# The down projections in square blocks, with Strassen's seven products in two of eleven super-groups

## The chip, the core and the metric

The kernel runs on one core of one Trainium2 chip. The time is the device time of one execution in microseconds (us). TensorE multiplies matrices, VectorE (DVE) and ScalarE (ACT) work on elements, GpSimd (POOL) does elementwise work too, and SyncE (SP) issues the loads. SBUF is the on-chip memory of 128 partitions, PSUM holds TensorE's results, and weights come from DRAM.

## The reference, cut to what matters

Two transformer blocks of width 2048 follow each other on 256 tokens: attention and a gated feed-forward network (1), then a gated recurrence and a gated feed-forward network (2), all in float32. The change is in the two down projections, the last products of the networks:

```
D_MODEL = 2048
SEQ = 256
D_FF = 5632
...
        u = causal_dwconv(h @ w_up[l], conv_w[l], conv_b[l])
        gate, up = jnp.split(u, 2, axis=-1)
        y = (jax.nn.gelu(gate, approximate=True) * up) @ w_down[l]
        x = x + rms_norm(y, post_ffn_norm[l])
...
    up = dwconv3(h @ w_in, w_conv)
    gate, val = jnp.split(up, 2, axis=-1)
    return (jax.nn.silu(gate) * val) @ w_out
```

So y (256 x 2048) is the hidden matrix (256 x 5632) times the weights (5632 x 2048). Its rows are normalised afterwards, which needs the sum of squares over all 2048 columns of a token.

## The kernel before, in words

The eight phases are called in1, out1, up1, down1, in2, out2, up2 and down2. All of them stream float32 weights in chunks of 256 rows and 512 columns (`raw`, 128 x 1024 elements, 512 KB) through a ring of four slots. Each chunk n is loaded by SP (`load`, L207), copied by ACT to `whi` (`split_hi`, L214, type fp32r), and VectorE writes the rest, raw minus whi, to `wlo` (`split_lo`, L219). TensorE then multiplies in three terms, high by high, high by low and low by high: for each of two 128-row tiles (`k`) and two token tiles (`t`) three matmuls of 128x512 output, twelve in a chunk (`products`, L232 to L234).

Four semaphores tie this together. A load into a slot waits until `lo_done` says that wlo of the chunk four before is done. `split_hi` waits until the chunk has landed and until `chunk_used` says that TensorE has used chunk n-4. `split_lo` waits for `hi_done`, and TensorE waits for `lo_done`.

A down projection has four groups of 512 output columns. For each group TensorE goes through all 44 row tiles (22 chunks) and gathers in one of two accumulators `acc` (256 tokens x 512 columns, one PSUM bank for each token tile). While the next group runs in the other accumulator, VectorE scales the finished group by the norm's gain row into `ybuf` (`back_group_dve`, L481) and ACT squares it and sums the squares (`back_group_act`, L489); then `group_free` says that the accumulator is free. The last four chunks of the last group go by token (`last_products`, L404 to L406): all of token tile 0 (`token0`), then all of token tile 1. `last_act` (L419, L423) squares and takes the root, VectorE takes the reciprocal (L444), scales the last group (L438), and adds each piece to `x` (L537). After down1, `pre_pe_by_token` turns `x` for in2 (L318, L306), with transposes for filling (L295). After down2, `x` goes to the output.

The hidden matrix comes from the up projection, one super-group of 512 hidden columns after the other, eleven in all, 44.2 us each. ACT copies the halves out (L589), VectorE scales them (`evacuate` L644, `scaled` L649), ACT starts the convolution of three taps (`centre`, L598: gate half in `cvg`, up half in `cvu`), VectorE adds the other taps (`convolve`, L662), ACT applies gelu or silu (L604), and POOL multiplies `cvg` by `cvu` (L718) and splits the product into `hhi` (L720) and `hlo` (L722). `centre` of super-group i waits until POOL is done with super-group i-1 (`up_hid`). The work of the last super-group lies in the first steps of the down projection.

The order of the work of each engine is the order in which the code is written; nothing is scheduled at run time except by semaphores.

## Time and profile before

| | |
|---|---|
| median of 3 runs | 2511.09 us (2509.42 to 2518.72) |
| the profiled execution: its span | 2510.2 us |
| the profiled execution's own time beside its span | none is listed apart from the span; the span is 0.9 us under the median |
| TensorE busy | 2496.8 us (99%), 15417 matmuls |
| VectorE busy | 1656.4 us (66%) |
| ACT busy | 1336.6 us (53%) |
| POOL busy | 221.3 us (9%) |
| DRAM read | 458.40 MB, 183 GB/s over the span |

The busy time of an engine is the union of its instructions. A matmul's duration in the profile (0.39 us for 128x512) is longer than the distance between two starts, since matmuls overlap; what one costs is read from the starts, or from a stretch divided by its count.

### The profile page before, as it was taken

To read this page: it belongs to the slowest core of one execution; us is meant where nothing else is said; L and a number is where in the kernel's file an instruction comes from. 1 tells how busy PE (TensorE), PEld (TensorE's weight loads), DVE (VectorE), ACT (ScalarE), POOL (GpSimd) and SP (SyncE) were. 2 spreads that over 40 slices of the span, in tenths; PEclk is the share of its full clock that TensorE was granted. 3 is DMA by queue.
4 is the path that set the end of the run, shared out by engine and by line. 5 is a ranking of instruction groups with operands and counts; after the bars stand their busy time and mean duration, and the time that the engine had idled before them with its cause. 6 is when DMAs were issued, how large, how long until landed. Compare 5 with 4: busy or idle time off the path is not lost.

```text
span 2510.2 us, 40508 instructions
## 1 busy us (share of the span) xinstructions
PE 2496.8 (99%) x15417; PEld 2153.2 (86%) x15417; DVE 1656.4 (66%) x2020; ACT 1336.6 (53%) x1754; POOL 221.3 (9%) x96
## 2 busy tenths in 40 slices
PE   9999999999999999999999999999999999999998
PEld 9999988888888888888888888888888888888887
DVE  6665675776777775445495968775677777775444
ACT  6554564656565554445545455454656556554343
POOL 1000000031211211000000000000012131221000
PEclk9999999999999999999999999999999999999999
DMA  7865445566666666555655655545566666666554
GB/s 236 254 206 154 118 140 185 180 190 188 189 186 191 192 188 210 195 194 187 193 173 164 176 154 174 160 149 188 174 186 192 191 186 191 188 189 211 194 194 156
DMA packets 241720, 462.25 MB, mean 184 GB/s; under 512 B 14392, under 2 KB 23921, under 8 KB 240961
## 3 DMA queue, kind: packets, MB, share of 16 engines
q1 hardware_dynamic: 239937, 453.45, 58.9%
q0 software_dynamic: 1568, 7.10, 0.9%
q8 instruction: 85, 1.39, 0.2%
q14 instruction: 34, 0.28, 0.0%
q10 hardware_dynamic: 96, 0.02, 0.0%
HBM read 458.40 MB, written 2.12 MB: 183 GB/s over the span
## 4 chain that ended last, share of the span: by engine, by line
PE 98%; ACT 0%; DMA 0%; DVE 0%; issue 0%; SPq 0%; DVEq 0%; ACTq 0%
PE acc L232 13%; PE acc L252 13%; PE acc L233 13%; PE acc L234 13%; PE tp L252 13%; PE tp L254 7%; PE acc L254 7%; PE acc L967 2%; PE acc L969 2%; PE acc L970 2%; PE acc L1193 1%; PE acc L1195 1%; PE acc L1194 1%; PE tp L1696 1%; PE acc L975 1%; PE acc L977 1%
## 5 line engine op out<-in xcount | busy, mean ns | idle before, releaser
L219 DVE TENSOR_TENSOR wlo<-raw,whi 128x1024 fp32r<-128x1024 f32 x855 | 1073.8, 1263 | 725.9 <-ACT whi L214 724.3
L214 ACT ACTIVATE whi<-raw 128x1024 fp32r<-128x1024 f32 x855 | 902.5, 1059 | 991.1 <-PE acc L234 458.2
L252 PE MATMUL acc<-ahl,whi 128*128 128x512 f32 x1408 | 490.2, 392 | 0.6 <-DVE ahl L337 0.6
L252 PE MATMUL tp<-ahl,whi 128*128 128x512 f32 x1408 | 489.5, 391 | 0.0
L254 PE MATMUL tp<-ahl,wlo 128*128 128x256 f32 x1408 | 394.2, 280 | 0.0
L254 PE MATMUL acc<-ahl,wlo 128*128 128x256 f32 x1408 | 394.1, 280 | 0.0
L252 PEld LDWEIGHTS acc<-ahl,whi 128*128 128x128 f32 x1408 | 263.4, 187 | 59.0 <-issue 1.0
L252 PEld LDWEIGHTS tp<-ahl,whi 128*128 128x128 f32 x1408 | 263.3, 187 | 57.7
L232 PE MATMUL acc<-whi,ahl 128*128 128x512 f32 x752 | 298.7, 397 | 1.8 <-DVE ahl L1794 1.5
L234 PE MATMUL acc<-whi,ahl 128*128 128x512 f32 x752 | 293.0, 390 | 0.0
L233 PE MATMUL acc<-wlo,ahl 128*128 128x512 f32 x752 | 292.7, 389 | 0.0
L254 PEld LDWEIGHTS tp<-ahl,wlo 128*128 128x128 f32 x1408 | 266.1, 189 | 0.1
L254 PEld LDWEIGHTS acc<-ahl,wlo 128*128 128x128 f32 x1408 | 266.0, 189 | 0.0
L234 PE MATMUL acc<-whi,hlo 128*128 128x512 f32 x672 | 261.4, 389 | 0.0
L233 PE MATMUL acc<-wlo,hhi 128*128 128x512 f32 x672 | 261.4, 389 | 0.0
L232 PE MATMUL acc<-whi,hhi 128*128 128x512 f32 x672 | 261.4, 389 | 0.0
L718 POOL TENSOR_TENSOR cvg<-cvg,cvu 128x1024 f32<-128x1024 f32 x22 | 98.2, 4462 | 1485.8 <-DVE cvu L662 1485.8
L232 PEld LDWEIGHTS acc<-whi,ahl 128*128 128x128 f32 x752 | 141.2, 188 | 31.4 <-issue 2.8
L234 PEld LDWEIGHTS acc<-whi,ahl 128*128 128x128 f32 x752 | 141.2, 188 | 29.9
L233 PEld LDWEIGHTS acc<-wlo,ahl 128*128 128x128 f32 x752 | 141.3, 188 | 27.5
L967 PE MATMUL acc<-ahl,whi 128*128 128x256 f32 x512 | 151.4, 296 | 0.2 <-DVE wlo L1572 0.2
L234 PEld LDWEIGHTS acc<-whi,hlo 128*128 128x128 f32 x672 | 126.1, 188 | 26.4
(286 smaller groups left out, 2963.8 us busy)
## 6 DMA issues: line engine op xcount, KB each, us to landing
raw<-in_w_up_dram SPq DMA_DIRECT2D x176, 512.0 KB, 4.1
raw<-in_ffn_w_in_dram SPq DMA_DIRECT2D x176, 512.0 KB, 4.2
raw<-in_hgrn_w_in_dram SPq DMA_DIRECT2D x160, 512.0 KB, 3.6
raw<-in_w_down_dram SPq DMA_DIRECT2D x88, 512.0 KB, 3.9
raw<-in_ffn_w_out_dram SPq DMA_DIRECT2D x88, 512.0 KB, 3.7
raw<-in_w_in_dram SPq DMA_DIRECT2D x87, 512.0 KB, 4.1
raw<-in_w_out_dram SPq DMA_DIRECT2D x32, 512.0 KB, 3.6
raw<-in_hgrn_w_out_dram SPq DMA_DIRECT2D x32, 512.0 KB, 3.8
```

Of the source, the lines that this page charges most:

```text
L214: act.activation(whi[:, s, :], raw[:, s, :], ACT.Copy).then_inc(hi_done, 1)
L219: dve.tensor_tensor(wlo[:, s, :], raw[:, s, :], whi[:, s, :].bitcast(F32), ALU.subtract).then_inc(lo_done, 1)
L232: pe.matmul(out[:, t, :], xh, whi[:, s, c], start=(kt == 0), stop=False)
L233: pe.matmul(out[:, t, :], xh, wlo[:, s, c], start=False, stop=False)
L234: mm = pe.matmul(out[:, t, :], xl, whi[:, s, c], start=False, stop=(kt == nk - 1))
L252: pe.matmul(o[:, ct % 2, :].rearrange("p (a t) -> p a t", a=2), whi[:, s, c], ahl[:, :, kt, :], start=(kt == 0), stop=False, skip_group_ch ...
L254: mm = pe.matmul(o[:, ct % 2, 0:S], wlo[:, s, c], ahi[:, kt, :], start=False, stop=(kt == KT - 1), skip_group_check=True)
L718: pool.tensor_tensor(cvg[:, :, :], cvg[:, :, :], cvu[:, :, :], ALU.mult).then_inc(sem(f"{ph}_pr"), 1)
L967: pe.matmul(o[:, d], whi[:, s, a], ahi[:, kt, :], start=first and ct % 2 == 0, stop=False, skip_group_check=True)
L969: pe.matmul(o[:, d], whi[:, s, a], alo[:, kt, :], start=False, stop=False, skip_group_check=True)
L970: mm = pe.matmul(o[:, d], wlo[:, s, a], ahi[:, kt, :], start=False, stop=last, skip_group_check=True)
L975: pe.matmul(out[:, t, :], xh, whi[:, s, a], start=first, stop=False)
```

## The change

The up projections' arithmetic, the attention and the recurrence stay. In a down projection:

- The loops are written out: 100 steps (`DOWN`) instead of 88 chunks. The output is made in two pairs of column groups (i = 0, 1); both accumulators are open at once. Super-groups of 512 hidden rows come in the order 0, 1, 2, 5, 3, 4, 6, 7, 8, 10, 9. One super-group and one pair is a square of 2 x 2 weight chunks (256 rows by 512 columns each).
- Nine super-groups (`R_SGS`) are regular: four steps of twelve matmuls (L552 to L554 of the changed kernel).
- Super-groups 5 and 10 (`S_SGS`) make seven block products, each a step of six matmuls (L566 to L568) with one token tile's worth of hidden blocks. Four of the steps use sums of weight chunks: `weight_sums` (L647) adds them in place in `raw`, two chunks at a time, and each sum is then split again into whi and wlo. A raw slot is free only after the last step that uses it, steps 3 to 6 (`FREED`).
- The hidden side: for these super-groups POOL's `seven_parts` makes the sums of hidden blocks and splits seven blocks, nine operations in place of two. Super-group 10 (`LATE`) goes through `down_pool`, after the load of the gain row.
- Products 1, 5, 6 and 7 gather in the two `tp` pairs of banks; the others go straight into the open accumulators. After super-group 10 ACT copies product 1 (L673), and VectorE forms U (L694), W (L705) and two more differences (L711, L718) and adds them to the four output blocks (L701, L707, L714, L720). The last super-group, 9, waits block by block for these additions (`down_last`): by columns, (token 0, columns 0), (1, 0), (0, 1), (1, 1), or in the last pair of down2 by token, (0, 0), (0, 1), (1, 0), (1, 1). Block 0 is the first of them.
- At the end of down1 and down2 two column groups are scaled, squared and added where there was one (`c1_act`, `c1_y`, `down_rest`).

The core of the diff:

```diff
+S_RAW = (0, 2, 3, 0, 1, 2, 3)
+S_A = (0, 6, 1, 4, 3, 5, 2)
+S_SGS = (5, 10)
...
+LATE = 10
+DOWN_ORDER = (0, 1, 2, 5, 3, 4, 6, 7, 8, 10, 9)
...
+        def back_load(sp, ph, w):
+            for m in range(M_DOWN):
...
+                    sp.wait_ge(lo_done, cb[ph] + FREED[m - RING] + 1)
...
+        def one_of_seven(pe, ph, d):
+
+            out = (P1B, cols(ph, 1)[:, 0, :], cols(ph, 0)[:, 0, :], P5B, P7B, P6B, cols(ph, 0)[:, 1, :])[d.j]
+            a = S_A[d.j]
...
+            for kk in range(CK):
+                w = slice(kk * GC, (kk + 1) * GC)
+                xh, xl = part7(d.sg, 0, a, kk), part7(d.sg, 1, a, kk)
+                pe.matmul(out, xh, whi[:, d.n % RING, w], start=fresh and kk == 0, stop=False, skip_group_check=True)
+                pe.matmul(out, xh, wlo[:, d.n % RING, w], start=False, stop=False, skip_group_check=True)
+                mm = pe.matmul(out, xl, whi[:, d.n % RING, w], start=False, stop=False, skip_group_check=True)
+            mm.then_inc(chunk_used, 1)
...
+            for b, (t, c) in enumerate(blocks_of(i, nxt)):
+                pe.wait_ge(sem("pre_sums"), 4 * (NPAIR * DOWNS.index(ph) + i) + b + 1)
...
+        def down_hi(act, ph, d):
+
+            n = cb[ph] + d.n
+            if d.summed and d.j >= 3:
+                act.wait_ge(sem("sums"), ub[ph] + SUMS[d.i, d.sg] + d.j - 2)
+            else:
+                act.wait_ge(landed[d.m % RING], 16 * ((rb[ph] + d.m) // RING + 1))
+            act.wait_ge(chunk_used, n - RING + 1)
+            act.activation(whi[:, d.n % RING, :], raw[:, d.m % RING, :], ACT.Copy).then_inc(hi_done, 1)
...
+        def weight_sums(dve, ph, d):
...
+            if d.j == 0:
+                dve.wait_ge(landed[1], 16 * ((rb[ph] + d.m + 1) // RING + 1))
+                add(0, 1)
+            if d.j == 1:
+                add(1, 2)
+            if d.j == 2:
+                dve.wait_ge(sem("sums"), s0 + 1)
+                add(2, 0)
+                dve.wait_ge(sem("sums"), s0 + 3)
+                add(3, 2)
...
+                if at == -1:
+                    sum_11(dve, ph, d.i)
+                if at == 1:
+                    sum_u(dve, ph, d.i)
+                    (sum_12 if by_token else sum_21)(dve, ph, d.i)
+                if at == 2 and not by_token:
+                    sum_12(dve, ph, d.i)
+                if at == 3:
+                    if by_token:
+                        sum_21(dve, ph, d.i)
+                        down_rest(dve, ph, k, 0)
+                    sum_22(dve, ph, d.i)
```

VectorE's order in down1 before, from the first chunk after the up projection's tail to the third group's scaling (`x18` is eighteen alike in a row):

```order
L219 TENSOR_TENSOR wlo<-raw,whi 128x1024 x18
L481 TENSOR_TENSOR ybuf<-acc,gbd 128x512 x2
L219 TENSOR_TENSOR wlo<-raw,whi 128x1024 x21
L481 TENSOR_TENSOR ybuf<-acc,gbd 128x512 x2
L219 TENSOR_TENSOR wlo<-raw,whi 128x1024 x23
```

The changed kernel, VectorE in down1, from the first sum of super-group 10 to the first output sums of the first pair:

```order
L647 TENSOR_TENSOR raw<-raw 128x1024
L639 TENSOR_TENSOR wlo<-raw,whi 128x1024
L647 TENSOR_TENSOR raw<-raw 128x1024
L639 TENSOR_TENSOR wlo<-raw,whi 128x1024
L647 TENSOR_TENSOR raw<-raw 128x1024 x2
L639 TENSOR_TENSOR wlo<-raw,whi 128x1024 x4
L701 TENSOR_TENSOR acc<-acc,ybuf 128x512
L639 TENSOR_TENSOR wlo<-raw,whi 128x1024 x2
L694 TENSOR_TENSOR ybuf<-tp,ybuf 128x512
L711 TENSOR_TENSOR ybuf<-tp,ybuf 128x512
L714 TENSOR_TENSOR acc<-acc,ybuf 128x512
L639 TENSOR_TENSOR wlo<-raw,whi 128x1024
```

Four sums of raw (L647) now stand between the wlo of the seven steps, and six more operations of 128x512 between the wlo of super-group 9.

POOL in the up projection's loop before, for one super-group:

```order
L718 TENSOR_TENSOR cvg<-cvg,cvu 128x1024
L720 ISA
L720 COPY hhi<-cvg 128x1024
L722 REGISTER_ALU
L722 TENSOR_TENSOR hlo<-cvg,hhi 128x1024
```

POOL of the changed kernel for super-group 5:

```order
L990 TENSOR_TENSOR cvg<-cvg,cvu 128x1024
L1011 TENSOR_TENSOR cvu<-cvg 128x512
L1013 CAST hsum<-cvg 128x512
L1014 CAST hsum<-cvg 128x256
L1016 TENSOR_TENSOR cvu<-cvg,cvu 128x256
L1018 TENSOR_TENSOR hsum<-cvg,hsum 128x512
L1020 TENSOR_TENSOR hsum<-cvg,hsum 128x256
L1022 TENSOR_TENSOR cvu<-cvg,cvu 128x256
L1024 CAST hsum<-cvu 128x1024
L1026 TENSOR_TENSOR hsum<-cvu,hsum 128x1024
```

The product (L718, now L990) stays, and a copy and a subtract have become nine operations. The same nine follow for super-group 10 after the load of `gbd`.

VectorE at the end of down1, before:

```order
L219 TENSOR_TENSOR wlo<-raw,whi 128x1024 x14
L444 RECIPROCAL prs<-prs 128x1
L537 SCALAR_TENSOR_TENSOR x<-ybuf,prs,x 128x512
L438 TENSOR_TENSOR ybuf<-acc,gbd 128x512
L219 TENSOR_TENSOR wlo<-raw,whi 128x1024
L537 SCALAR_TENSOR_TENSOR x<-ybuf,prs,x 128x512
L219 TENSOR_TENSOR wlo<-raw,whi 128x1024
L444 RECIPROCAL prs<-prs 128x1
L537 SCALAR_TENSOR_TENSOR x<-ybuf,prs,x 128x512
L438 TENSOR_TENSOR ybuf<-acc,gbd 128x512
L537 SCALAR_TENSOR_TENSOR x<-ybuf,prs,x 128x512
```

And in the changed kernel, from the last output sum on:

```order
L720 TENSOR_TENSOR acc<-acc,ybuf 128x512
L725 TENSOR_REDUCE prs<-psq 128x1
L727 TENSOR_SCALAR prs<-prs 128x1
L725 TENSOR_REDUCE prs<-psq 128x1
L727 TENSOR_SCALAR prs<-prs 128x1
L267 TENSOR_TENSOR wlo<-raw,whi 128x1024
L734 TENSOR_TENSOR ybuf<-acc,gbd 128x512 x2
L504 RECIPROCAL prs<-prs 128x1
L799 SCALAR_TENSOR_TENSOR x<-ybuf,prs,x 128x512 x2
L267 TENSOR_TENSOR wlo<-raw,whi 128x1024
L504 RECIPROCAL prs<-prs 128x1
L799 SCALAR_TENSOR_TENSOR x<-ybuf,prs,x 128x512
```

Two reductions by token and two scalings of the third group have moved behind the last wlo, and the first wlo of in2 has moved ahead of the reciprocal of token 0.

## Rows read from the trace of the kernel before

**Rows 1.** The page, part 1: busy us of each engine, share, instructions.

```profile
PE 2496.8 (99%) x15417; PEld 2153.2 (86%) x15417; DVE 1656.4 (66%) x2020; ACT 1336.6 (53%) x1754; POOL 221.3 (9%) x96
```

**Rows 2.** Windows of down1 and down2: span, busy of PE, PEld, DVE, ACT, POOL, PEclk, DMA.

```profile
930.90:1170.30 239.40, 239.40 (x1058) 198.16 (x1057) 118.08 (x109) 101.33 (x110) 9.97 (x4) 1.00 0.59 195
2262.90:2502.70 239.80, 239.76 (x1059) 198.18 (x1057) 118.30 (x111) 98.42 (x107) 9.96 (x4) 1.00 0.55 186
```

**Rows 3.** Timeline of PE and ACT in down1: start us, us, what [idle before, releaser].

```profile
933.66 0.39 PE L232 MATMUL acc<-whi,hhi 128*128 128x512 f32 x1
...
933.92 1.06 ACT L214 ACTIVATE whi<-raw 128x1024 fp32r<-128x1024 f32 x1 [0.73 <-PE acc L234]
...
955.68 1.06 ACT L214 ACTIVATE whi<-raw 128x1024 fp32r<-128x1024 f32 x1 [1.65 <-PE acc L234]
```

**Rows 4.** Timeline of DVE in up1.

```profile
903.60 2.35 DVE L219 TENSOR_TENSOR wlo<-raw,whi 128x1024 fp32r<-128x1024 f32 x2
...
916.89 1.21 DVE L649 TENSOR_TENSOR ut<-ut,uprow 128x1024 f32<-128x1024 f32 x1
```

**Rows 5.** An issue; landings of loads issued at 953.66, 969.51, 1004.41, 958.99.

```profile
955.64 0.37 SPq L207 DMA_DIRECT2D raw<-in_w_down_dram  x1
...
DMA to landing us min/median/max: 3.5/3.5/3.5
...
DMA to landing us min/median/max: 3.8/3.8/3.8
...
DMA to landing us min/median/max: 4.4/4.4/4.4
...
DMA to landing us min/median/max: 8.0/8.0/8.0
```

**Rows 6.** Chain at in2's first matmul, between DVE's ahl and TensorE.

```profile
1174.86 0.14 issue
```

**Rows 7.** Timeline of DVE and ACT at the first group's end in down1.

```profile
993.28 1.28 DVE L481 TENSOR_TENSOR ybuf<-acc,gbd 128x512 f32<-128x512 f32 x2
...
995.79 2.00 ACT L214 ACTIVATE whi<-raw 128x1024 fp32r<-128x1024 f32 x2
```

**Rows 8.** Timeline of POOL and of DVE in the first steps of down1.

```profile
947.97 4.45 POOL L718 TENSOR_TENSOR cvg<-cvg,cvu 128x1024 f32<-128x1024 f32 x1 [34.41 <-DVE cvu L662]
952.60 1.81 POOL L720 CAST hhi<-cvg 128x1024 f32 x1 [0.17 <-POOL cvg L718]
954.57 3.18 POOL L722 TENSOR_TENSOR hlo<-cvg,hhi 128x1024 f32 x1 [0.17 <-POOL hhi L720]
...
947.80 2.36 DVE L219 TENSOR_TENSOR wlo<-raw,whi 128x1024 fp32r<-128x1024 f32 x2
...
951.34 2.16 DVE L219 TENSOR_TENSOR wlo<-raw,whi 128x1024 fp32r<-128x1024 f32 x1 [1.18 <-ACT whi L214]
954.06 1.42 DVE L219 TENSOR_TENSOR wlo<-raw,whi 128x1024 fp32r<-128x1024 f32 x1 [0.56 <-ACT whi L214]
956.78 2.05 DVE L219 TENSOR_TENSOR wlo<-raw,whi 128x1024 fp32r<-128x1024 f32 x1 [1.30 <-ACT whi L214]
```

**Rows 9.** Timeline of DVE and ACT around a super-group's change in up1.

```profile
912.79 1.85 DVE L219 TENSOR_TENSOR wlo<-raw,whi 128x1024 fp32r<-128x1024 f32 x1 [1.50 <-ACT whi L214]
...
922.63 3.47 DVE L662 SCALAR_TENSOR_TENSOR cvg<-ut,taps,cvg 128x255 f32<-128x255 f32 x8
...
918.43 2.08 ACT L598 ACTIVATE cvg<-ut,taps 128x256 f32<-128x256 f32 x4
```

**Rows 10.** Timeline of ACT and DVE at the end of down1.

```profile
1165.77 1.28 ACT L423 ACT_TABLE_LOAD   x1
...
1168.26 0.68 DVE L438 TENSOR_TENSOR ybuf<-acc,gbd 128x512 f32<-128x512 f32 x1
...
1171.98 0.75 DVE L537 SCALAR_TENSOR_TENSOR x<-ybuf,prs,x 128x512 f32<-128x512 f32 x1
```

**Rows 11.** Timeline of DVE at the end of down2.

```profile
2505.22 2.07 DVE L537 SCALAR_TENSOR_TENSOR x<-ybuf,prs,x 128x512 f32<-128x512 f32 x3
```

More of the change, by code:

```diff
@@ new lines, in bass_two_blocks, with blocks_of, part7, regular @@
+        BY_TOKEN = ((0, 0), (0, 1), (1, 0), (1, 1))
+        BY_COLUMNS = ((0, 0), (1, 0), (0, 1), (1, 1))
+        def blocks_of(i, nxt):
+            return BY_TOKEN if i == NPAIR - 1 and not nxt else BY_COLUMNS
+        def part7(sg, lo, a, kk):
+            if sg == LATE:
+                return hlate[:, lo, 2 * a + kk, :]
+            return hsum[:, lo, 2 * a + kk, :]
+        def regular(pe, ph, d):
+            r, c = RC[d.j]
+            for kk in range(CK):
+                kt, w = 4 * R_SGS.index(d.sg) + CK * r + kk, slice(kk * GC, (kk + 1) * GC)
+                first = d.sg == DOWN_ORDER[0] and r == 0 and kk == 0
+                for t in range(NT):
+                    xh, xl = hhi[:, kt, t * P:(t + 1) * P], hlo[:, kt, t * P:(t + 1) * P]
+                    pe.matmul(cols(ph, c)[:, t, :], xh, whi[:, d.n % RING, w], start=first, stop=False, skip_group_check=True)
+                    pe.matmul(cols(ph, c)[:, t, :], xh, wlo[:, d.n % RING, w], start=False, stop=False, skip_group_check=True)
+                    mm = pe.matmul(cols(ph, c)[:, t, :], xl, whi[:, d.n % RING, w], start=False, stop=False,
+                                   skip_group_check=True)
+            mm.then_inc(chunk_used, 1)
@@ new lines, in down_last @@
+        def down_last(pe, ph, i, n, sg, nxt):
+            for b, (t, c) in enumerate(blocks_of(i, nxt)):
+                pe.wait_ge(sem("pre_sums"), 4 * (NPAIR * DOWNS.index(ph) + i) + b + 1)
+                for r in range(2):
+                    s = (n + 2 * c + r) % RING
+                    if t == 0:
+                        pe.wait_ge(lo_done, cb[ph] + n + 2 * c + r + 1)
+                    for kk in range(CK):
+                        kt, w = 4 * R_SGS.index(sg) + CK * r + kk, slice(kk * GC, (kk + 1) * GC)
+                        xh, xl = hhi[:, kt, t * P:(t + 1) * P], hlo[:, kt, t * P:(t + 1) * P]
+                        pe.matmul(cols(ph, c)[:, t, :], xh, whi[:, s, w], start=False, stop=False, skip_group_check=True)
+                        pe.matmul(cols(ph, c)[:, t, :], xh, wlo[:, s, w], start=False, stop=False, skip_group_check=True)
+                        mm = pe.matmul(cols(ph, c)[:, t, :], xl, whi[:, s, w], start=False,
+                                       stop=(r == 1 and kk == CK - 1), skip_group_check=True)
+                    if t:
+                        mm.then_inc(chunk_used, 1)
+                if i == NPAIR - 1 and t == 0:
+                    mm.then_inc(sem("token0") if c else sem("down_c1"), 1)
@@ new lines, in back_pe @@
+        def back_pe(pe, ph, k, ready, nxt):
+            pe.wait_ge(ready, FG)
+            pe.wait_ge(group_free, gb[ph] - 1)
+            for d in DOWN:
+                if d.i and d.sg == DOWN_ORDER[0] and d.j in (0, 2):
+                    group(pe, gb[ph] + 2 * d.i + RC[d.j][1])
+                if d.summed and d.n == DOWN_FIRST_SUM:
+                    pe.wait_ge(group_free, gb[ph])
+                if d.sg == LATE and d.i == 0 and d.j == 0:
+                    pe.wait_ge(ready, FG + 1)
+                if d.last:
+                    if d.j == 0:
+                        down_last(pe, ph, d.i, d.n, d.sg, nxt)
+                else:
+                    pe.wait_ge(lo_done, cb[ph] + d.n + 1)
+                    (one_of_seven if d.summed else regular)(pe, ph, d)
@@ new lines, in down_lo, with add @@
+        def down_lo(dve, ph, d):
+            dve.wait_ge(hi_done, cb[ph] + d.n + 1)
+            dve.tensor_tensor(wlo[:, d.n % RING, :], raw[:, d.m % RING, :], whi[:, d.n % RING, :].bitcast(F32),
+                              ALU.subtract).then_inc(lo_done, 1)
+        def weight_sums(dve, ph, d):
+            s0 = ub[ph] + SUMS[d.i, d.sg]
+            def add(to, other):
+                dve.tensor_tensor(raw[:, to, :], raw[:, to, :], raw[:, other, :], ALU.add).then_inc(sem("sums"), 1)
+            if d.j == 0:
+                dve.wait_ge(landed[1], 16 * ((rb[ph] + d.m + 1) // RING + 1))
[7 more added lines that the diff above has]
+                add(3, 2)
```

323 lines of the change are left out of this document (236 added, 87 removed).

## The prediction

> **What bounds the kernel now.** I read the page first: TensorE is busy 99% of the span, VectorE 66%, ACT 53% [rows 1]. A microsecond saved on TensorE is a microsecond of the result only while its operands keep coming, so the question is what else is nearly late. The stretches that the change rewrites are the two down projections, 930.90 to 1170.30 us and 2262.90 to 2502.70 us. TensorE has no gap in them, and its granted clock is 1.00, the 2.4 GHz level [rows 2]. The first holds 1056 matmuls of its own (1058 less two of the up projection), so one costs 239.4/1056 = 0.227 us, a step of twelve 2.72 us, a step of six 1.36 us.
>
> Then I read how a weight chunk reaches TensorE. ACT copies chunk n to whi once step n-4 has freed the slot, 0.3 us later (step 1 begins at 933.66, the copy at 933.92) [rows 3]; VectorE starts wlo 1.10 us after the copy started (955.68, 956.78) [rows 3, 8]. Two wlo in a row take 2.35 us: 1.23 for one, 1.14 from start to start [rows 4]. The reload of raw is issued 0.15 us after the wlo that frees it (955.48, 955.64). It lands after 3.5 or 3.8 us where the queue had been quiet for over 3 us, after 4.4 in the normal rhythm, and after 8.0 beside the 1 MB gain row [rows 5]. In that rhythm wlo is ready some 5.5 us ahead (three steps of 2.72 less 0.3, less 2.3 from the copy's start to the end of wlo). From VectorE's result to a matmul that waits for it I count 0.3 us (0.14 of issue and a weight load) [rows 6].
>
> **What is removed.** Two super-groups in each of two column pairs make seven block products of six matmuls instead of eight: 24 matmuls in a down projection, 48 in all, 48 x 0.227 = 10.9 us. That is 0.43%, and the most that the change can give. About 0.5% (12.6 us) is what a measurement of this kernel tells from no change.
>
> **Added in a super-group of seven.** Its steps last 7 x 1.36 = 9.52 us on TensorE. VectorE has seven wlo and four sums of raw, which no row shows; the nearest, a product of the same 128x1024 f32, takes 1.21 [rows 4], so 11 x 1.14 = 12.5 us. It falls 3 us behind, inside the lead of 5.5, but then the reload counts. Let 0 be TensorE's start of the first of the seven, s0. The copy for s2 waits for the step before last of the group ahead (ends at -2.72) and starts at -2.42, wlo(s2) at -1.31, the last two sums at -0.17 and 1.08, wlo(s3) runs from 2.22 to 3.45. TensorE wants it at 4.08: in time. But only wlo(s3) frees the first raw slot, where before every step freed one. Issue at 3.60, landing x later, 0.02 to the copy, 1.11 to wlo, 1.23 for it, 0.3 to the matmul: 6.26 + x. TensorE is through at 9.52, so it waits x - 3.26. The queue has been quiet for over 3 us there, hence x = 3.8 and 0.54 us. Eight such places (a regular super-group follows each): 4.3 us. Ends: 1.9 at 3.5, 9.1 at 4.4.
>
> **The combination.** From the start of the first wlo after super-group 10: two wlo 2.28, three PSUM operations at 0.7 each with their own waits 2.1, 0.25 to TensorE = 4.63. TensorE wants block 1 at 1.53 + 2.72 = 4.25: a wait of 0.38, three times (PSUM rows: 1.28 for two [rows 7]). In the last pair of down2 the blocks go by token and block 1 needs a wlo that stands behind U, W and a sum: 5.85 against 4.25, 1.6. Between the pairs, both output banks end at nearly one time; the first is free after two ybuf products (1.28) and two squares (ACT goes on 1.2 later) [rows 7], behind the late sums: about 0.4, once per down. Together 1.1 + 1.6 + 0.8 = 3.5 us. Before, the second bank hid all this. The ends are 0 (combination 1 us sooner, 0.4 left in down2) and 5.
>
> **POOL.** A cast and a subtract become nine operations for super-groups 5 and 10: 2816 columns of sums, 1792 of casts. By the durations of the rows (3.18 and 1.81 per 1024) they take 8.7 + 3.2 + 0.9 of gaps = 12.8 us. Laid beside VectorE's rows, though, the same rows show waits [rows 8]: the product at 947.97 ends 2.27 us after a pair of wlo (950.15); wlo at 951.34 ends 1.08 after that product; the cast at 952.60 ends 0.91 after that wlo; the subtract at 954.57 ends 2.27 after the next wlo (955.48); wlo at 956.78 ends 1.08 after the subtract. So each waits for the other's whole instruction, a cast is really 0.9 and a sum 2.27 per 1024, and VectorE back to back keeps POOL out.
>
> The Trainium skill (SBUF — State Buffer, "SBUF: two separate sides") has this as a rule: the port pair that VectorE and GpSimd share is a lock held for a whole instruction, also by a VectorE operation with two SBUF inputs against a GpSimd operation that reads SBUF. By that rule, the five ends above agree; by it the sum below stands at +5.5, and with the plain durations at -0.9, since both POOL terms go.
>
> In the up projection, 44.2 us ahead of those rows in the same rhythm, super-group 5 then runs: sum 909.3 to 910.5; casts behind the delayed wlo to 912.4; add to 913.15, under the wlo at 912.79; subtract 914.3 to 915.45 beside the evacuation; next to 916.1; VectorE busy (wlo, scale, wlo) to 919.5; add 920.1; cast 921.15; last subtract 923.6 [rows 9]. ACT's centre of the next group waits for it: it ran at 918.43 for 2.08, now from 923.65. Copy to 926.7, wlo to 927.9, convolution (3.47) to 931.3, next wlo to 932.5, matmul at 932.8, where TensorE wants it at 930.9: 1.9 us, two times, 3.8. Ends 0 (by 921.2 nothing is late) and 6.
>
> In each down, super-group 10's parts start at 952.4 and reach into the first super-group of seven (930.90 + 12 x 2.72 = 963.5). Three POOL operations come ahead of VectorE, 1.4 us in all, so wlo(s3) ends at 968.3: a wait of 1.0 there and 0.9 at the reload instead of 0.54. Extra 1.3, twice, 2.6. If the last subtract (2.27) also beats the reloaded chunk's wlo, which by my times it misses by 0.2 us, it is 3.6 each, 7.2. The lower end is 0.
>
> **The two ends.** The last four steps of a down went by token, with token 0 complete 5.4 us early, and its square, table load (1.28) and root beneath the rest [rows 10]. In down1 they go by columns now: token 0 is complete 2.72 us early, its root ready at the end - 0.2, two adds to +1.5, a wlo, token 1's first add to +3.6. Before it ended at 1172.73, +2.4 [rows 2, 10]. The turning for the next projection starts 1.3 us later. In down2 the last square waits for VectorE's fourth ybuf product, 1.4 us, but then four adds follow the root instead of five operations (0.75 + 0.6 + 2.07 [rows 10, 11]): 0.9 later. Together 2.2; ends 0 and 4. The gain row is now loaded at 931 instead of 957. I cost that at nothing: the chunks issued there are wanted 8.4 us later, against 8.0 [rows 5], and the lead of 5.5 covers the rest; uncovered it would be 1 us. The unrolled loops also cost nothing.
>
> **Sum.** -10.9 + 4.3 + 3.5 + 3.8 + 2.6 + 2.2 = +5.5 on the profiled span of 2510.2. The median of the runs, 2511.09, stands 0.9 above that span: 2516.6, said as 2517.
>
> **The rivals.** (a) My forecast: waits of 11 to 23 us swallow the saving, 2511 to 2523. 0.62. (b) The waits are mostly covered: reloads land in 3.5, POOL gets its slots sooner. 1.9 + 1.5 + 2.2 and nothing from POOL leaves 5.3 us of gain, 2506, and with everything hidden 2500. For it: VectorE is busy for only 118 of 239 us in a down [rows 2]; against it, that is a mean, and each super-group of seven asks for 12.5 in 9.5. 0.20. (c) It ends slower: the reload decides, at x - 3.26 in eight places. From x = 4.7 (8 x 1.44 = 11.5 in place of 4.3, sum +12.7) it passes 0.5%; at 5 it is 13.9, +15.1, 2526. For it: 4.4 is normal, and four reloads now follow at 1.14 us; against it: TensorE waits for the first alone. 0.15. (d) The change doesn't do what it says: steps of six matmuls cost TensorE as much as before for the group, nothing is saved, 2516.6 + 10.9 = 2527.5. No row speaks for it: matmuls of all three lines follow at 0.227. 0.03.
>
> **How the numbers follow.** The bounds of all terms at once give 2500 and, with 9.1 + 5 + 6 + 7.2 + 4, 2531. Half of (b), and half of (c) and (d), lie inside 2504 to 2526. Faster by over 0.5% (under 2498.5) is more than the matmuls can give: 0.03 for what I overlook. Slower is most of (c) and (d): 0.16. Within: 0.81.
>
> **What would show it.** 24 matmuls fewer in each down; down1's stretch at 239.4 - 5.4 + 2.2 + 0.8 + 0.4 + 1.3 = 238.7 us. Right: TensorE gaps of 0.5 us before the first regular step after each seven, twice that around the first; sums of raw at 1.14; ACT's centre after super-group 5 waiting some 5 us for POOL. Wrong, and towards (b): no gaps there, or POOL's nine within 13 us. Towards (c): reloads of 4.4 and more with gaps above 1 us, or sums over 1.3 us, each 0.1 of which adds 0.4 per place.

## The result, and the profile after

The changed kernel took 2531.6 us in the median of five runs (2531.09 to 2542.79), the kernel before 2512.12 us beside it. The ratio is 1.0086, with a 95% interval from 1.0061 to 1.0111. That is slower, by more than the 0.5% that can be told from no change, and outside the range that was given. A second set of four runs, beside the kernel before again, gave 1.0092 (1.0062 to 1.0123).

The first line of the page of the changed kernel answers to [rows 1]:

```profile
PE 2505.8 (99%) x15369; PEld 2146.8 (85%) x15369; DVE 1758.8 (69%) x2112; ACT 1362.8 (54%) x1782; POOL 258.8 (10%) x124
```

TensorE does 48 matmuls less and is busy 9 us longer. Windows of up1, down1, up2 and down2 show where (length, then busy time and count of PE, PEld, DVE, ACT, POOL, granted clock, DMA); the two down projections answer to [rows 2]:

```profile
437.50:937.06 499.56, 499.55 (x2835) 433.99 (x2835) 361.28 (x433) 290.81 (x351) 100.65 (x37) 1.00 0.62 185
937.06:1184.49 247.43, 238.98 (x1034) 194.77 (x1032) 163.17 (x152) 114.44 (x124) 20.47 (x11) 0.99 0.56 188
1787.97:2283.21 495.24, 494.17 (x2834) 433.31 (x2835) 355.25 (x433) 291.10 (x351) 104.72 (x37) 1.00 0.63 186
2283.21:2528.68 245.47, 237.94 (x1034) 194.04 (x1032) 162.39 (x150) 112.29 (x121) 20.49 (x11) 0.99 0.53 181
```

The kernel before, its up1 (up2 took 490.60 too):

```profile
440.30:930.90 490.60, 490.57 (x2834) 432.55 (x2835) 353.56 (x433) 291.64 (x351) 94.49 (x30) 1.00 0.63 188
```

So the profiled execution (span 2538.7, 28.5 more than before) lost 8.0 us in down1 (238.7 had been forecast for this stretch), 5.7 in down2, 9.0 in up1 and 4.6 in up2, 1.1 and 2.5 at the two ends, and 0.4 elsewhere between down1 and up2. It gained 2.8 ahead of up1, where nothing was changed; there the kernel before had a stretch at a granted clock of 0.50, 3.4 us from 239.9, and the changed kernel had none. What TensorE waited for in down1 and down2 of the changed kernel, by the view of waits (total, times, longest; the kernel before has no such line in down1):

```profile
PE tp L566 <- DVE wlo L639: 3.9, 1, 3.9
PE acc L582 <- DVE wlo L639: 2.6, 2, 1.3
PE acc L552 <- DVE wlo L639: 1.0, 1, 1.0
...
PE tp L566 <- DVE wlo L639: 3.9, 1, 3.9
PE acc L582 <- DVE wlo L639: 3.2, 3, 1.6
```

The first line is the largest, and it stands in both: the fourth product of the first seven, which is the group of seven made from super-group 5 in the first pair. Below, a wait is the distance of two starts less 0.227 us, and the first and the second chunk are those that TensorE uses first behind a group of seven.

**The first seven.** TensorE in down1:

```profile
973.58 0.39 PE L568 MATMUL acc<-whi,hsum 128*128 128x512 f32 x1
977.84 0.79 PE L566 MATMUL tp<-whi,hsum 128*128 128x512 f32 x1 [3.87 <-DVE wlo L639]
978.43 0.63 PE L567 MATMUL tp<-wlo,hsum 128*128 128x512 f32 x1
978.85 0.63 PE L568 MATMUL tp<-whi,hsum 128*128 128x512 f32 x1
```

It stands idle for 4.03 us, and then the matmuls follow at 0.43 instead of 0.23 us. The windows of PE (busy, granted clock, DMA) say why: 0.50 is the 1.2 GHz level.

```profile
977.00:980.00 3.00, 2.17 (x5) 0.50 0.29 85
980.00:983.00 3.00, 3.00 (x8) 0.50 0.92 296
```

That costs another 2.6 us here. In down2 the idle time is 4.02 us and the slow matmuls behind it cost 1.7. The prediction had a wait of 1.0 us at this place and no slow matmuls. VectorE and POOL just before, which answer to [rows 8] (in both, a time can include waiting for the other engine):

```profile
962.92 1.56 DVE L639 TENSOR_TENSOR wlo<-raw,whi 128x1024 fp32r<-128x1024 f32 x1 [1.04 <-ACT whi L634]
964.40 2.32 DVE L647 TENSOR_TENSOR raw<-raw 128x1024 f32<-128x1024 f32 x1
966.64 1.75 DVE L639 TENSOR_TENSOR wlo<-raw,whi 128x1024 fp32r<-128x1024 f32 x1
968.32 1.75 DVE L647 TENSOR_TENSOR raw<-raw 128x1024 f32<-128x1024 f32 x1
970.00 2.06 DVE L639 TENSOR_TENSOR wlo<-raw,whi 128x1024 fp32r<-128x1024 f32 x1
971.98 3.41 DVE L647 TENSOR_TENSOR raw<-raw 128x1024 f32<-128x1024 f32 x1
975.42 1.22 DVE L647 TENSOR_TENSOR raw<-raw 128x1024 f32<-128x1024 f32 x1
976.56 2.35 DVE L639 TENSOR_TENSOR wlo<-raw,whi 128x1024 fp32r<-128x1024 f32 x2
...
963.36 2.28 POOL L1018 TENSOR_TENSOR hlate<-cvg,hlate 128x512 fp32r<-128x512 f32 x1
965.60 1.72 POOL L1020 TENSOR_TENSOR hlate<-cvg,hlate 128x256 fp32r<-128x256 f32 x1
967.27 1.72 POOL L1022 TENSOR_TENSOR cvu<-cvg,cvu 128x256 f32<-128x256 f32 x1
969.06 1.92 POOL L1024 CAST hlate<-cvu 128x1024 fp32r<-128x1024 f32 x1
971.06 3.25 POOL L1026 TENSOR_TENSOR hlate<-cvu,hlate 128x1024 fp32r<-128x1024 f32 x1
```

VectorE has next to no idle time from 962.92 on, yet up to 975.39 a POOL operation ends between every two of its own: 1.5 to 2.2 us from start to start instead of 1.14, and 3.4 around POOL's last and longest. The two behind it take 1.14 again. The fourth wlo is over at 977.79 (976.56 + 1.23), 0.05 before the matmul.

**The reload.** ACT in front of super-group 9 in down1 (four loads were issued at 1165.07, 1166.20, 1167.34, 1168.48), and the first two loads' times from issue to landing:

```profile
1168.72 1.06 ACT L634 ACTIVATE whi<-raw 128x1024 fp32r<-128x1024 f32 x1 [1.66 <-DMA raw<-in_w_down_dram]
1171.77 1.06 ACT L634 ACTIVATE whi<-raw 128x1024 fp32r<-128x1024 f32 x1 [1.99 <-DMA raw<-in_w_down_dram]
...
DMA to landing us min/median/max: 3.6/3.6/3.6
...
DMA to landing us min/median/max: 5.5/5.5/5.5
```

The first lands after 3.6 us, near the 3.5 and 3.8 of [rows 5]; the second, 1.13 us behind it in issue, lands after 5.5, so 3.1 us after the first. TensorE starts on the first chunk at 1171.18, and in super-group 9 a block takes only six matmuls from a chunk: it wants the second one 1.4 us later, not 2.72, and waits 1.50 us. The matmul that waited there, and the one that waited most for a first chunk, behind super-group 5:

```profile
1174.14 0.50 PE L582 MATMUL acc<-whi,hhi 128*128 128x512 f32 x1 [1.33 <-DVE wlo L639]
...
1107.12 0.50 PE L552 MATMUL acc<-whi,hhi 128*128 128x512 f32 x1 [1.04 <-DVE wlo L639]
```

At 1107.12 the first of the four loads (issued at 1099.82) had landed after 4.9 us. With the somewhat slower matmul behind each, the waits behind a seven come to 7.4 us over both downs: 5.3 at second chunks, all four of them behind super-group 10 (1.5, 1.6, 1.1, 1.1), and 2.1 at first chunks, 1.3 of it at 1107.12.

**The up projection.** POOL's product of hidden blocks runs once in a super-group; two of them in up1, two in up2 ahead of super-group 5, and two behind it:

```profile
547.47 4.39 POOL L990 TENSOR_TENSOR cvg<-cvg,cvu 128x1024 f32<-128x1024 f32 x1 [36.36 <-DVE cvu L924]
592.70 4.39 POOL L990 TENSOR_TENSOR cvg<-cvg,cvu 128x1024 f32<-128x1024 f32 x1 [35.30 <-DVE cvu L924]
...
1896.39 4.39 POOL L990 TENSOR_TENSOR cvg<-cvg,cvu 128x1024 f32<-128x1024 f32 x1 [34.65 <-DVE cvu L924]
1940.76 4.40 POOL L990 TENSOR_TENSOR cvg<-cvg,cvu 128x1024 f32<-128x1024 f32 x1 [34.64 <-DVE cvu L924]
...
2119.99 4.39 POOL L990 TENSOR_TENSOR cvg<-cvg,cvu 128x1024 f32<-128x1024 f32 x1 [26.92 <-DVE cvu L924]
2164.99 4.39 POOL L990 TENSOR_TENSOR cvg<-cvg,cvu 128x1024 f32<-128x1024 f32 x1 [35.28 <-DVE cvu L924]
```

A super-group takes 45.23 us in all of up1, 44.37 in up2 up to super-group 5, and 45.2 behind it, at a granted clock of 1.00 throughout. Where up2 changes, ACT's centre waits for POOL's last operation, and TensorE once for the wlo that ACT's delay makes late (1.07 us at 2102.2). In up1, slower from its start, the centre waited 3.5 us and TensorE not at all. The centre in up2:

```profile
2093.32 2.08 ACT L860 ACTIVATE cvg<-ut,taps 128x256 f32<-128x256 f32 x4 [4.97 <-POOL hsum L1026]
```

The super-groups of both up projections took 44.4 us before (the 44.2 given ahead of the prediction for all eleven is that of the last alone). A whole up projection at the slower rhythm costs 9.0 us, which is about the distance between the two groups of single runs: 2540.5 and 2542.8 (the profiled one is among them) against 2531.1 to 2531.6, and before 2518.7 and 2520.0 against 2509.4 to 2512.1. That the groups differ by this rhythm fits their times; no trace of the shorter runs of the changed kernel shows it.

### The profile page after: what moved, and what is told of

The parts are those of the page before. It is cut to its first block, busy times and chain, and to the rows that moved or that the text cites. A ratio compares the mean times of both kernels' runs of the same rounds, so it can differ in the third digit from the quotient of the medians.

```text
span 2538.7 us, 39934 instructions
## 1 busy us (share of the span) xinstructions
PE 2505.8 (99%) x15369; PEld 2146.8 (85%) x15369; DVE 1758.8 (69%) x2112; ACT 1362.8 (54%) x1782; POOL 258.8 (10%) x124
## 4 chain that ended last, share of the span: by engine, by line
PE 92%; DVE 4%; ACT 1%; POOL 1%; issue 1%; DMA 1%; DVEq 0%; ACTq 0%; POOLq 0%
PE acc L300 12%; PE tp L300 12%; PE acc L280 7%; PE acc L282 7%; PE acc L281 7%; PE acc L302 6%; PE tp L302 6%; PE acc L552 4%; PE acc L553 4%; PE acc L554 4%; PE acc L1277 2%; PE acc L1279 2%; PE acc L1280 2%; DVE wlo L639 2%; PE acc L1503 1%; PE acc L1505 1%
## 5 line engine op out<-in xcount | busy, mean ns | idle before, releaser
L267 DVE TENSOR_TENSOR wlo<-raw,whi 128x1024 fp32r<-128x1024 f32 x695 | 882.8, 1279 | 510.3 <-ACT whi L262 505.5
L262 ACT ACTIVATE whi<-raw 128x1024 fp32r<-128x1024 f32 x693 | 731.4, 1059 | 758.4 <-PE acc L302 225.1
L300 PE MATMUL acc<-ahl,whi 128*128 128x512 f32 x1408 | 496.2, 397 | 1.6 <-DVE wlo L267 1.1
L300 PE MATMUL tp<-ahl,whi 128*128 128x512 f32 x1408 | 495.9, 397 | 0.0
L639 DVE TENSOR_TENSOR wlo<-raw,whi 128x1024 fp32r<-128x1024 f32 x184 | 229.1, 1257 | 153.0 <-ACT whi L634 152.3
L634 ACT ACTIVATE whi<-raw 128x1024 fp32r<-128x1024 f32 x186 | 197.0, 1060 | 238.9 <-PE acc L554 177.0
L990 POOL TENSOR_TENSOR cvg<-cvg,cvu 128x1024 f32<-128x1024 f32 x22 | 96.5, 4388 | 1449.4 <-DVE cvu L924 1449.4
L552 PE MATMUL acc<-whi,hhi 128*128 128x512 f32 x512 | 199.9, 390 | 1.2 <-DVE wlo L639 1.0
L553 PE MATMUL acc<-wlo,hhi 128*128 128x512 f32 x512 | 199.5, 390 | 0.0
L554 PE MATMUL acc<-whi,hlo 128*128 128x512 f32 x512 | 199.4, 389 | 0.0
```

What stands on the lines that cost most here:

```text
L262: act.activation(whi[:, s, :], raw[:, s, :], ACT.Copy).then_inc(hi_done, 1)
L267: dve.tensor_tensor(wlo[:, s, :], raw[:, s, :], whi[:, s, :].bitcast(F32), ALU.subtract).then_inc(lo_done, 1)
L300: pe.matmul(o[:, ct % 2, :].rearrange("p (a t) -> p a t", a=2), whi[:, s, c], ahl[:, :, kt, :], start=(kt == 0), stop=False, skip_group_ch ...
L552: pe.matmul(cols(ph, c)[:, t, :], xh, whi[:, d.n % RING, w], start=first, stop=False, skip_group_check=True)
L553: pe.matmul(cols(ph, c)[:, t, :], xh, wlo[:, d.n % RING, w], start=False, stop=False, skip_group_check=True)
L554: mm = pe.matmul(cols(ph, c)[:, t, :], xl, whi[:, d.n % RING, w], start=False, stop=False, skip_group_check=True)
```

## The experiments

**1. Super-group 5 later.**

```diff
-DOWN_ORDER = (0, 1, 2, 5, 3, 4, 6, 7, 8, 10, 9)
+DOWN_ORDER = (0, 1, 2, 3, 4, 6, 5, 7, 8, 10, 9)
```

> Super-group 5 takes the seventh place of the order (0, 1, 2, 3, 4, 6, 5, 7, 8, 10, 9), some 32 us later, when GpSimd's parts of super-group 10 are over. Nothing else changes. Theory A (GpSimd's operations take turns with VectorE's and so make the fourth wlo of the first seven late): TensorE's wait of 4.39 us in down1 and 4.02 in down2 goes, and with it the slow matmuls behind it (2.23 and 1.68 us at a granted clock of 0.5). In their place comes the reload wait of 0.7 to 1.5 us at the first matmuls after that group. down1's stretch 247.4 - 6.6 + 1.3 = 242.1 us, down2's 245.5 - 5.7 + 1.0 = 240.8; the time 10 us under the changed kernel's, 2521. Rival B (eleven VectorE operations for a group of 9.5 us are too many wherever the group stands): the wait moves with the group, 3 us and more at the fourth product, and the time stays at 2531.

Measured: 2522.05 us (2521.38 to 2522.89), ratio 1.0044 (1.0031 to 1.0058), 9.5 us under the changed kernel. TensorE does not wait in the first seven of down1, and the granted clock stays at 1.00 in both downs:

```profile
935.89:1175.04 239.15, 236.60 (x1034) 192.76 (x1032) 160.21 (x153) 114.47 (x124) 18.61 (x11) 1.00 0.58 195
2270.11:2511.05 240.94, 236.13 (x1034) 192.85 (x1032) 159.77 (x150) 112.29 (x121) 18.65 (x11) 1.00 0.55 185
```

Theory A holds and rival B falls: away from POOL, eleven VectorE operations in 9.5 us are covered by the lead, as the prediction had it. The wait at the first chunk that appears behind the group was 0.2 us in down1, where that load landed after 3.8 us, and 1.6 in down2, where it took 5.2.

**2. POOL's nine operations as two.**

```diff
-            pool.tensor_tensor(sums[:, 0:4, :].rearrange("p (b k) c -> p b k c", b=2), a11_a22, a21_a21, ALU.subtract)\
...
-            pool.tensor_copy(to[:, 0, 6:14, :], sums).then_inc(sem("seven_s"), 1)
+            pool.tensor_copy(hi, cvg[:, :, :]).then_inc(sem("seven_s"), 1)
             pool.wait_ge(sem("seven_s"), j + 1)
-            pool.tensor_tensor(to[:, 1, 6:14, :], sums, to[:, 0, 6:14, :].bitcast(F32), ALU.subtract)\
-                .then_inc(sem(f"{ph}_hid"), 1)
+            pool.tensor_tensor(lo, cvg[:, :, :], hi.bitcast(F32), ALU.subtract).then_inc(sem(f"{ph}_hid"), 1)
```

> GpSimd's nine operations for super-groups 5 and 10 are replaced by one cast and one subtract of 128x1024 as in the other super-groups; the six blocks of sums on the hidden side are filled with zeros once, so the seven products are made from other numbers. All else stays, the order too. Theory A: TensorE's waits at the first seven (4.39 and 4.02) and the slow matmuls behind them (2.23, 1.68) go, a reload wait of about 1.3 comes in their place in each down; the wait of 1.07 us in up2 behind the centre goes. Down1 242.1, down2 240.8 us. If a wait of TensorE also turns the rhythm of the up projection from 44.4 to 45.2 us a super-group (theory R), up2 stays at 44.4 to its end, 3.5 us less, and the time is 2531 - 10.3 - 1.1 - 3.5 = 2516; if the rhythm is drawn at random (rival R0), up1 or up2 may be at either, and the time is 2520 with single runs 9 us above. Rival B (VectorE is too slow for seven whatever GpSimd does): the waits at the fourth product stay at 3 us and more.

Measured: 2517.04 us (2514.15 to 2524.95, ten runs), ratio 1.0023 (1.0014 to 1.0033). With the order of the changed kernel the waits at the first seven are gone, and the sums run at their own pace:

```profile
965.58 1.22 DVE L647 TENSOR_TENSOR raw<-raw 128x1024 f32<-128x1024 f32 x1
966.72 1.21 DVE L639 TENSOR_TENSOR wlo<-raw,whi 128x1024 fp32r<-128x1024 f32 x1
```

From the first wlo's start to the fourth's end it is 10.5 us, against 14.9 in the changed kernel. The downs took 239.34 and 241.13. No up projection has a wait, and none changes its rhythm; but up1 ran at 45.2 us from its first super-group in the profile, so a rhythm is also drawn at the beginning, without this change.

**3. Smaller loads behind a seven.**

```diff
+                rows = 1 if m >= RING and q and DOWN_ORDER[p0] in S_SGS else CK
+                sp.dma_start(raw[:, m % RING, 0:rows * GC].rearrange("p (k c) -> p k c", k=rows),
+                             (w_tile(w, CK * (2 * sg + r), i * (2 * GC) + c * GC) if rows == CK else
+                              w_half(w, CK * (2 * sg + r), i * (2 * GC) + c * GC))).then_inc(landed[m % RING], 16)
```

> The second, third and fourth chunk loaded after a group of seven products are loads of 256 KB in place of 512 KB (their first row tile; the other half of the slot keeps old numbers). The first of the four stays whole. Theory C (four loads that follow at 1.14 us share the transfer rate, so the second lands 5.5 us after its issue and TensorE waits inside the next group's first step pair): the second chunk's landing falls to 4.5 us or less, the waits for its wlo (1.54, 1.31, 1.60 us in down1; 1.07, 0.18, 1.07 in down2; 6.8 in all) go to under 0.2 each, the time falls by 6 to 7 us to 2525. Rival D (the second chunk is late by the order of ACT's copies and VectorE's operations, not by its landing): the waits stay within 0.3 us of what they were.

Measured: 2528.3 us (2523.55 to 2532.16, four runs), ratio 1.0063 (1.0048 to 1.0078). The waits at second chunks fell from 5.3 us to 0.4. Those at first chunks, whose loads stayed whole, were 1.1, of which 0.8 stand behind super-group 5 in down1's second pair, at a load that landed after 4.4 us. In front of super-group 9 in down1 ACT's last three copies now follow in one row, and the first of them waited 0.52 us where it was 1.99 above:

```profile
1165.54 2.96 ACT L641 ACTIVATE whi<-raw 128x1024 fp32r<-128x1024 f32 x3 [0.52 <-DMA raw<-in_w_down_dram]
```

So for the second chunk the landing decides (theory C), not the order of ACT and VectorE. The two downs of the profiled run (2532.16) took 485.9 us together, against 492.9, which is the 6 to 7 us expected. The median fell by 3.3 us only: in the profiled run both up projections changed to the slower rhythm behind super-group 5, and the four runs scatter over 9 us.

**4. Sums of weights made tiny.**

```diff
-                dve.tensor_tensor(raw[:, to, :], raw[:, to, :], raw[:, other, :], ALU.add).then_inc(sem("sums"), 1)
+                dve.tensor_tensor(raw[:, to, 0:8], raw[:, to, 0:8], raw[:, other, 0:8], ALU.add).then_inc(sem("sums"), 1)
+            dve.wait_ge(lo_done, cb[ph] + d.n + 1)
```

> The four sums of weight chunks per group of seven are made over 8 of 1024 columns only, with a wait for the wlo ahead of them, so four of the seven products take other weights; the number of copies, wlo, matmuls and loads stays, GpSimd's nine operations too. It takes 4 x 1.2 us of VectorE out of each group. Theory E (VectorE's eleven operations in 9.5 us are what starves both places): the waits at the first seven go (no 4.39, 4.02, no clock of 0.5), the loads behind a seven are issued about 1.36 us apart and 0.9 us sooner, and the waits there (6.8 and 0.6 us in all) go to under 1 in all; the time is 2531 - 12.3 - 6.5 = 2512. Rival (GpSimd alone, or the transfers alone decide): at least one of the two kinds of wait stays over 1 us at its place, the time at 2518 or above.

Measured: 2522.96 us (2520.88 to 2523.63, four runs), ratio 1.0047 (1.0031 to 1.0062); downs 239.49 and 239.64. Half of theory E failed. The wait at the first seven went (0.2 left), so it takes both, POOL's turns and VectorE's sums. Waits behind a seven stayed, 4.8 us: 2.7 at second chunks and 2.1 at first ones. Behind super-group 10 in down1 the loads were issued 1.43 us apart (1033.04, 1034.47, 1035.90); the first two landed after

```profile
DMA to landing us min/median/max: 3.7/3.7/3.7
...
DMA to landing us min/median/max: 5.6/5.6/5.6
```

and the third after 6.1. So the second load lands late without VectorE's sums too, also at a wider spacing.

**5. The kernel before, with more work for POOL.**

```diff
-            with pool.Fori(0, FG) as i:
+            for i in range(FG):
...
+                if i == 5:
+                    for r in range(EXTRA):
+                        pool.tensor_tensor(cvu[:, 0:2, :], cvg[:, 0:2, :], cvg[:, 2:4, :], ALU.subtract)\
+                            .then_inc(sem(f"{ph}_extra"), 1)
```

> The kernel before, with nothing of the change but five more subtracts of 128x512 by GpSimd between the product and the cast of super-group 5 in each up projection (their result is used by nobody), so that the centre of the next super-group waits for GpSimd. Theory R (a wait of TensorE of about 1 us draws the matmul rhythm anew): in each up projection the period from the sixth to the seventh product grows by 1 to 1.8 us over 44.37, and in at least one of them the periods behind it are 45.2 instead of 44.37 us, 3 to 4 us more; the time is 2514 to 2522. Rival R0 (the rhythm has nothing to do with waits): the periods behind the wait are as those ahead of it in both, the time is 2513 to 2514.

Measured: 2520.38 us (2517.65 to 2529.48, ten runs), ratio 1.0037 (1.0024 to 1.005): 8.7 us out of POOL's work in the up projections alone. The products in up2 of the profiled run:

```profile
2059.53 4.39 POOL L719 TENSOR_TENSOR cvg<-cvg,cvu 128x1024 f32<-128x1024 f32 x1 [34.65 <-DVE cvu L663]
2106.50 4.38 POOL L719 TENSOR_TENSOR cvg<-cvg,cvu 128x1024 f32<-128x1024 f32 x1 [26.68 <-DVE cvu L663]
2151.73 4.39 POOL L719 TENSOR_TENSOR cvg<-cvg,cvu 128x1024 f32<-128x1024 f32 x1 [36.37 <-DVE cvu L663]
```

Here TensorE waited 1.4 and 0.4 us in each up projection, which adds 2.6 to that period, more than I had expected. Behind it up2 went on at 45.2 us and up1 at 44.4. R0 falls: the rhythm changed at the wait. (The edit also writes POOL's loop out; this was not tried without the extra work.)

**6. The centre freed,** on top of experiment 1's order. GpSimd's sums go to `hscr`, and `hid` is signalled when cvg has been read last.

```diff
-            sums = cvu[:, :, :].rearrange("p k (h c) -> p (k h) c", h=2)
+            sums = hscr[:, :, :]
...
+            m = pool.tensor_tensor(to[:, 1, 4:6, :], cvg[:, 2:4, tok1], to[:, 0, 4:6, :].bitcast(F32), ALU.subtract)
+            if i != LATE:
+                m.then_inc(sem(f"{ph}_hid"), 1)
```

> The order with super-group 5 in seventh place, and GpSimd's sums of hidden blocks go to a buffer of their own in place of cvu. The three sums stand ahead of the two subtracts, and the centre of the next super-group waits only for the subtract that reads cvg last, two operations of 128x1024 earlier than before. Theory (GpSimd's nine operations reach TensorE only through this wait of the centre): the centre waits under 1.5 us in place of 5, TensorE does not wait in the up projections, all eleven periods are alike in each; the time falls from 2522 by the 1.3 and 5.5 us that the two up projections lost there, to 2515 to 2518. Rival (GpSimd slows VectorE's wlo by taking turns, centre or not): a wait of TensorE over 0.5 us stays in the up projections, the time stays at 2521 to 2522.

Measured: 2518.15 us (2513.3 to 2527.84, twelve runs), ratio 1.0024 (1.0012 to 1.0037), just above what was expected and widely scattered. The centre waits for its own input now, not for POOL, and TensorE has no wait in either up projection:

```profile
2085.68 2.08 ACT L861 ACTIVATE cvg<-ut,taps 128x256 f32<-128x256 f32 x4 [0.79 <-DVE ut L912]
```

In the profiled run up1 went at 45.2 us from its first super-group and up2 at 44.4 to its end.

**7. A fifth slot for the reload,** on top of experiment 6. The first chunk behind a seven gets a slot of its own, `xraw`, and is loaded earlier.

```diff
+        XS = [m for m in range(RING, M_DOWN) if m % 4 == 0 and DOWN_ORDER[(m - RING) // 4 % FG] in S_SGS]
...
+                elif in_x(m):
+                    sp.wait_ge(chunk_used, cb[ph])
+                    sp.wait_ge(hi_done, cb[ph] + min(d.n for d in DOWN if d.m == m - RING) + 1)
...
+                sp.dma_start(raw_of(m).rearrange("p (k c) -> p k c", k=CK),
```

> As the run before, and the first chunk after each group of seven goes to a fifth slot of raw, loaded as soon as ACT has copied the first chunk of the seven, so that only three loads follow closely behind the seven and the one that lands late is the third chunk of the next group, not the second. Theory C (the second of closely spaced loads lands after 5.5 us and more, and TensorE wants it at once): the waits at the first and second chunk after a seven, 6.8 us in the run with super-group 5 in seventh place, go to under 1 us in all; what is left in the two down projections is the combination (0.57 and 0.11 three times, 1.8 once, 0.35 at each pair's change). The time is 2509 to 2511. Rival D (the order of ACT and VectorE makes the second chunk late): the waits move to the next chunk and stay over 3 us in all, the time 2514 and more.

Measured: 2510.37 us (2506.48 to 2518.06, twelve runs), ratio 0.9995 (0.998 to 1.001).

```profile
932.21:1168.56 236.35, 235.15 (x1034) 193.23 (x1032) 159.79 (x152) 114.46 (x124) 18.50 (x11) 1.00 0.58 198
2262.28:2499.10 236.82, 234.90 (x1034) 193.23 (x1032) 159.27 (x150) 112.22 (x121) 18.52 (x11) 1.00 0.54 188
```

Behind a seven 0.7 us of waiting is left in all. The downs now take 3 us less each than in [rows 2], of 5.4 that the matmuls save; the rest is the combination. The runs form two groups, seven from 2506.5 to 2511.0 and five from 2515.5 to 2518.1; before, 26 of 29 lie from 2509.4 to 2513.5 and three from 2519.3 to 2521.8. The lowest is 2.9 us under the lowest of before; as a whole it cannot be told from it.

**8. The combination made tiny**, on top of experiment 7: the copy and eight VectorE operations over 8 of 512 columns.

```diff
-            dve.tensor_tensor(U7, P6B, Q7, ALU.subtract).then_inc(sem("down_u"), 1)
+            dve.tensor_tensor(U7[:, 0:8], P6B[:, 0:8], Q7[:, 0:8], ALU.subtract).then_inc(sem("down_u"), 1)
```

> The kernel with the fifth slot, and of the combination behind super-group 10 only 8 of 512 columns are computed (the copy of product 1, the four differences and the four additions to the output blocks); their order and waits stay. The output lacks the rest of the seven products. Theory (the combination costs TensorE only what VectorE's nine operations of 128x512 take ahead of a block): the waits at blocks 1 (0.58, 0.66, 0.68 us in three pairs, 1.87 in the last of down2) go to under 0.1 each, the 0.35 at each pair's change stays or halves; the two down projections take 234.1 to 234.8 us each, and the time falls by 3.8 us to 2502.7 in its fastest runs, 2506.5 in the median. Rival (the waits come from the wlo of the last super-group or from semaphores): half of them or more stay.

Measured: 2505.22 us (2502.92 to 2516.45, ten runs), ratio 0.9963 (0.9944 to 0.9982); downs 234.71 and 235.25. The waits at block 1 in three pairs and at the pairs' change went. In the last pair of down2 1.3 of 1.9 us stayed, against the expectation; ACT's copy of the third chunk there shows why:

```profile
2482.56 1.06 ACT L651 ACTIVATE whi<-raw 128x1024 fp32r<-128x1024 f32 x1 [1.76 <-DMA raw<-in_ffn_w_out_dram]
```

By token the second block wants the third chunk 1.5 us after the second, and here that one is the second of closely spaced loads. In the kernel of experiment 7 most of this wait is the reload's, not the combination's.

**9. The changed kernel again.**

> The changed kernel once more, for a second profile. Theory A: TensorE's waits at the fourth product of the first seven are 4.0 to 4.4 us again in both down projections, each with 10 to 12 slow matmuls behind it; the second chunks of the groups after a seven wait for 0.9 to 1.6 us again at most places. Theory R: an up projection that begins in periods of 44.4 us waits 1 us behind super-group 5 and may then go on at 44.4 or at 45.2; one that begins at 45.2 does not wait and stays. Rival R0: periods change at places without a wait too. Time 2531 to 2532, single runs up to 2541.

Measured: 2538.99 us (2535.34 to 2544.36, four runs), ratio 1.0092, above what was expected. The waits at the first seven were 4.04 and 4.03 us, the slow matmuls cost 1.7 each, the waits behind a seven 5.0 in all, 3.6 of it at second chunks. Both up projections began at 44.4 us and both changed to 45.2 behind the wait after super-group 5. Of the 13 runs of the kernel before beside it, six took 2521.2 to 2522.8, the others 2510.7 to 2513.8.

## Why the prediction was wrong

What held: 24 matmuls less in each down; the landing of the first reload, in seven of eight places (3.6 to 4.2 for a forecast of 3.8); VectorE's sums at 1.14 and their cover by the lead, away from POOL; the centre's wait of 5 us (4.97), with 1.07 us of TensorE's time for a forecast of 1.9, in one up projection of the profiled run.

The terms of the sum, forecast and measured in the profiled run:

| | forecast | measured |
|---|---|---|
| matmuls saved | -10.9 | -10.9 |
| POOL at the first seven: waits | +2.6 | +8.05 |
| matmuls at the 1.2 GHz level behind them | none | +4.35 |
| reload | +4.3 | +7.4 |
| combination and pairs' change | +3.5 | +4.6 |
| up projections | +3.8 | +4.6 in up2, +9.0 in up1 |
| the two ends | +2.2 | +3.6 |

With the 2.8 gained ahead of up1 and 0.4 lost between down1 and up2, the right column gives 28.3 of the 28.5 us. By their times the runs near the median are those without up1's 9.0.

**The step that failed first** is "VectorE back to back keeps POOL out". I let three POOL operations come ahead, 1.4 us in all; in the trace all five that were left came in, one between every two of VectorE's, and from the first wlo to the end of the fourth it took 4.4 us more than in experiment 2. Experiments 1, 2 and 4 each take that wait away, by its place, by POOL's side and by VectorE's, so this is shown. The five ends of [rows 8] gave the mutual exclusion but no case in which both had work queued, and I took the favourable reading. The price was bounded at 7.2, which the waits alone pass.

The Trainium skill (SBUF — State Buffer, "SBUF: two separate sides") gives the exclusive lock for a whole instruction. The changed kernel's trace agrees: VectorE's sum at 971.98 ends at 975.39, 1.08 us after POOL's subtract (971.06 + 3.25). So does experiment 2, with 1.14 us from start to start once POOL is done.

**The clock** had no term at all. Each idle time of 4.0 us was followed by 8 to 14 matmuls at the 1.2 GHz level; waits of 1.8 us and less were not. A wait of this size was paid 1.4 to 1.7 times.

**The reload** was mis-sized in its second chunk. The prediction said that "TensorE waits for the first alone", since later ones have 2.72 us more. Two numbers of that were wrong. The second of four loads at 1.14 us lands 2.5 to 3.1 us after the first behind super-group 10, and there TensorE wants it after six matmuls, 1.4 us. Behind super-group 5, where a step takes twelve, the second chunk cost nothing in the changed kernel and at most 0.3 us in any run here. Experiments 3, 4 and 7 show that the lateness is the transfer's. The kernel before had a small sign of it: a load issued at 999.39, 1.13 us behind another, landed after 4.36 us, the other after 3.82. The first chunks cost 2.1 us in all where 4.3 was forecast, and 1.3 of it at one place. Rival (c) had the right steps, but priced the first load, and its x rose at that place alone, to 4.9 us; in the four other profiles with this order the same load landed after 4.3 to 5.1. Why it is late there is open.

**The up projections**: POOL's nine operations cost TensorE a wait of 1 us, which I had as 1.9, and a new rhythm, which I had not. Over the eleven profiles here, 11 waits of TensorE behind super-group 5 were followed by the slower rhythm eight times; 11 up projections without such a wait never changed theirs. Experiment 5 produces both in the kernel before. The change itself is shown; why TensorE settles in one rhythm or the other is open.

**The combination** was right in its three small waits (0.68 for 0.38). The last pair's 1.84 for 1.6 has the cause that was forecast. ACT has copied the third chunk by 2517.61, and its wlo stands behind U, W and a sum:

```profile
2516.55 1.06 ACT L634 ACTIVATE whi<-raw 128x1024 fp32r<-128x1024 f32 x1 [0.74 <-DMA raw<-in_ffn_w_out_dram]
...
2518.43 0.70 DVE L707 TENSOR_TENSOR acc<-acc,ybuf 128x512 f32<-128x512 f32 x1
2519.03 2.35 DVE L639 TENSOR_TENSOR wlo<-raw,whi 128x1024 fp32r<-128x1024 f32 x2
```

Without them the wlo could start at about 2517.65, which would leave some 0.3 us of the wait (an estimate from these rows). Experiment 8 found mostly the reload at this place, but in a kernel whose fifth slot makes this chunk the late second load. The ends were 1.1 for 1.3, and 2.5 for 0.9. At the end of down2 four scaled additions follow the last root (2.74 us), as forecast; ACT's last square starts at 2531.13, behind VectorE's product of 2530.35, and that stands behind token 0's reciprocal, for which VectorE had waited 2.42 us. This was not tried by itself.
